# Down products of four feed-forward stages by Strassen's scheme, with the operand differences formed on GpSimd

## The reference, cut to what matters

```
def conv_ffn(x, w_up, conv_k, conv_b, w_down):          # layers of the first model
    h = x @ w_up                                         # 512 x 5632
    h = sum(hp[:, j:j + S] * conv_k[j] for j in range(CONV_W)) + conv_b
    a, b = jnp.split(h, 2, axis=-1)
    return (jax.nn.gelu(a, approximate=False) * b) @ w_down   # 512 x 2816 @ 2816 x 1024

def swiglu(xn, w_gate, w_up, w_down):                    # layers of the second model
    return (jax.nn.silu(xn @ w_gate) * (xn @ w_up)) @ w_down  # the same sizes
```

## Time and profile before

| | |
|---|---|
| time, median of 3 runs (lowest, highest) | 3466.81 us (3466.40, 3467.09) |
| span of the profiled execution | 3464.9 us |
| PE busy | 3404.4 us, 98% |
| DVE busy | 1870.3 us, 54% |
| ACT busy | 1401.5 us, 40% |
| POOL busy | 252.1 us, 7% |

### The profile page before, as it was taken

How to read it: one execution, slowest core, us unless ns; L and a number is a source line. 1 busy time by engine, 2 the same in 40 slices (tenths; PEclk the granted TensorE clock), 3 DMA queues, 4 the chain that set the end, 5 groups by cost and what they waited for, 6 DMA issues and landing times.

```text
span 3464.9 us, 41693 instructions
## 1 busy us (share of the span) xinstructions
PE 3404.4 (98%) x16871; PEld 2849.4 (82%) x16871; DVE 1870.3 (54%) x3030; ACT 1401.5 (40%) x2489; POOL 252.1 (7%) x319
## 2 busy tenths in 40 slices
PE   9999999999999999999999999999999999999999
PEld 8888888888888888888888777888888887888887
DVE  5644566646565545676455695553333696543332
ACT  4543233424235333334243554544232565543231
POOL 1300210000032002000001020100000000100000
PEclk9999999999999999999999999999999999999999
DMA  4111342322331123423232222412222302313222
GB/s 160 56 55 62 109 158 73 104 97 92 98 105 60 49 86 114 141 68 103 98 98 77 75 71 90 132 57 96 98 97 98 104 28 90 105 55 108 95 96 79
DMA packets 89330, 315.13 MB, mean 91 GB/s; under 512 B 10673, under 2 KB 11441, under 8 KB 88625
## 3 DMA queue, kind: packets, MB, share of 16 engines
q1 hardware_dynamic: 89136, 312.46, 27.4%
HBM read 308.23 MB, written 4.19 MB: 90 GB/s over the span
## 4 chain that ended last, share of the span: by engine, by line
PE 88%; DVE 7%; ACT 2%; POOL 2%; issue 1%; DMA 0%; SPq 0%; DVEq 0%; ACTq 0%; POOLq 0%
PE bk L1182 76%; PE bk L1276 3%; PE bk L1240 2%; PE bk L1250 1%; PE bk L1196 1%; DVE ar L2165 1%; DVE wl L1792 1%; DVE st L2163 1%; PE bk L1367 1%; PE bk L1365 1%; PE bk L1366 1%; POOL x L2354 1%; POOL st L2286 1%; DVE x L1821 0%; DMA wr<-in_wpk 0%
## 5 line engine op out<-in xcount | busy, mean ns | idle before, releaser
L1182 PE MATMUL bk<-xh,wh 128*128 128x512 f32 (+1 forms) x2216 | 837.8, 378 | 5.1 <-DVE xl L1805 5.1
L1182 PE MATMUL bk<-xh,wl 128*128 128x512 f32 (+1 forms) x2216 | 830.3, 375 | 0.0
L1182 PE MATMUL bk<-xl,wh 128*128 128x512 f32 (+1 forms) x2216 | 829.6, 374 | 0.0
L1792 DVE TENSOR_TENSOR wl<-wr,wh 128x1024 fp32r<-128x1024 f32 (+1 forms) x372 | 449.4, 1218 | 660.7 <-ACT wh L1438 659.7
L1438 ACT ACTIVATE wh<-wr 128x1024 fp32r<-128x1024 f32 (+1 forms) x372 | 385.8, 1046 | 706.4 <-PE bk L1182 653.6
L1182 PEld LDWEIGHTS bk<-xh,wh 128*128 128x128 f32 x2216 | 417.5, 188 | 78.6 <-DVE wl L1798 3.8
L1182 PEld LDWEIGHTS bk<-xh,wl 128*128 128x128 f32 x2216 | 417.2, 188 | 75.3
L1182 PEld LDWEIGHTS bk<-xl,wh 128*128 128x128 f32 x2216 | 417.6, 188 | 72.0
L1182 PE MATMUL bk<-wh,ah 128*128 128x512 f32 x1184 | 466.6, 394 | 4.5 <-DVE al L2250 2.9
L1182 PE MATMUL bk<-wh,al 128*128 128x512 f32 x1184 | 461.7, 390 | 0.0
L1182 PE MATMUL bk<-wl,ah 128*128 128x512 f32 x1184 | 461.3, 390 | 0.0
(11 more groups left out here) (276 smaller groups left out, 4095.5 us busy)
## 6 DMA issues: line engine op xcount, KB each, us to landing
wr<-in_wpk SPq DMA_DIRECT2D x540, 512.0 KB, 3.4
gb<-in_ln_g SPq DMA_DIRECT2D x6, 512.0 KB, 4.5
gb<-in_ln_b SPq DMA_DIRECT2D x6, 512.0 KB, 6.0
ar<-in_xT SPq DMA_DIRECT2D x8, 256.0 KB, 6.5
wr<-in_wpk SPq DMA_DIRECT2D x8, 256.0 KB, 6.0
ar<-in_memT SPq DMA_DIRECT2D x2, 1024.0 KB, 5.0
x<-in_x SPq DMA_DIRECT2D x4, 512.0 KB, 5.3
park<-x SPq DMA_DIRECT2D x4, 512.0 KB, 6.2
```

The source lines that it names most:

```text
L1182: i = pe.e.matmul(dst, lw, rw, start=g not in opened, stop=end)
L1792: dve.e.tensor_tensor(m.wl[:, s, a], m.wr[:, r, a], m.wh[:, s, a].bitcast(F32), ALU.subtract) \
```

## The change

The down products are done in four phases per stage instead of two, on pairs of chunks: phase 0 after three up groups on pairs 0 and 1, phase 1 after two more groups on pairs 2 to 4, phases 2 and 3 after three groups each on pairs 5 to 7 and 8 to 10. A pair's activations are four blocks of 128 features by 256 rows of x, its weights (now one DMA of 1 MB into a new buffer `wd`, 88 units of `wpk` less) four blocks of 128 by 512. `Seven` and `seven` make seven block products, named by their number in the order 1, 5, 2, 6, 3, 7, 4, where eight stood before. A product of all pairs of a phase is two parts: (q, 0) on the first two pairs, (q, 1) on the third (phase 0 has two pairs, so no second part). In the first three products all first parts come before the second ones. Each part is one unit of the five pairs `wh`, `wl`.

- `comb` (POOL, four instructions of 128x256 per pair) forms the sums and differences of the activations, `combo` (POOL, four of 128x512 per pair, T1 to T4) those of the weights.
- `hid_hi` (ACT) and `hid_lo` (DVE) split the seven left operands of a pair: 1792 columns for 1024 before.
- `sev` (DVE) adds a product's two banks to x after each product, two for product 7: 16 additions per phase, 64 per stage. Product 6 adds onto the bank of product 1, 7 onto that of 6, 3 onto that of 5, so PE waits for the additions of the earlier one (`AFTER`).
- In the last phase the products 2 and 3 finish row tiles 0 and 1, product 4 the tiles 2 and 3.

The core of the diff:

```diff
+LEFT = {1: 0, 5: 4, 2: 2, 6: 5, 3: 6, 7: 1, 4: 3}
+RIGHT = {1: 0, 5: 1, 2: 2, 6: 1, 3: 3, 7: 0, 4: 2}
+COMBO = {5: "T1", 6: "T2", 7: "T3", 4: "T4"}
+HOME = {1: "a", 6: "a", 7: "a", 5: "b", 3: "b", 2: "c", 4: "d"}
+PART = {1: ((0, 0),), 5: ((1, 1),), 2: ((0, 0),), 6: ((0, 1),), 3: ((0, 1),), 7: ((1, 1), (1, 0)), 4: ((1, 0),)}
+AFTER = {6: 1, 7: 6, 3: 5}
...
+    def seven(self, F):
+        n = len(F.chunks)
+        order = [(q, c) for c in range(n) for q in (1, 5, 2)] + [(q, c) for q in (6, 3, 7) for c in range(n)]
+        combos = {(1, 0): (("T2", 0), ("T3", 0)), (5, 0): (("T4", 0),), (2, 0): (("T2", 1), ("T3", 1)),
+                  (1, 1): (("T4", 1),)} if n > 1 else {}
...
+        for q, c in order:
+            product(q, c, (0, 1), True)
+            for name, cc in combos.get((q, c), ()):
+                for pair in F.chunks[cc] if cc < n else ():
+                    self.add("combo", F, name, pair)
+            if c == n - 1:
+                for tt in range(2):
+                    self.out_of(F, q, tt)
...
+            self.tick()
...
+                self.add("comb", si, pair)
+                self.soon += [("hid_hi", si, pair), ("hid_lo", si, pair)]
+            drive((self.seven(F), 1))
...
+    def smm(F, q, c, tiles, fin):            # PE
+        pe.wait_ge(*ev["w_lo", j])
+        for tt in tiles:
...
+            if q in AFTER:
+                pe.wait_ge(*ev["sev", F.si, F.ph, AFTER[q], tt])
+            for kk, pair in enumerate(F.chunks[c]):
+                pe.wait_ge(*ev["hid", F.si, pair])
...
+    def split_seven(j):                      # ACT
+        act.wait_ge(*ev["used", j - NR])
+        for pair in F.chunks[c]:
+            act.wait_ge(*ev[(COMBO[q], F.si, pair) if q in COMBO else ("d_sw", F.si, pair)])
...
+    def comb(si, pair):                      # POOL
+        for p in range(2):
+            pool.wait_ge(*ev["prod", si, 2 * pair + p])
...
+        pool.e.tensor_tensor(zx[:, 0, :], z[:, 1, :], z[:, 3, :], ALU.add).then_inc(*ev.up("pool_ev"))
+        own()
+        pool.e.tensor_tensor(zx[:, 1, :], zx[:, 0, :], z[:, 0, :], ALU.subtract).then_inc(*ev.up("pool_ev"))
+        pool.e.tensor_tensor(z[:, 1, :], z[:, 0, :], z[:, 1, :], ALU.subtract).then_inc(*ev.up("pool_ev"))
+        own()
+        pool.e.tensor_tensor(zx[:, 2, :], z[:, 2, :], zx[:, 1, :], ALU.subtract) \
+            .then_inc(*ev.up("pool_ev", ("comb", si, pair)))
+    def combo(F, name, pair):                # POOL
+        w = m.wd[:, F.pairs.index(pair)]
+        dst, x, y = {"T1": (1, 1, 0), "T2": (1, 3, 1), "T3": (0, 1, 0), "T4": (2, 2, 1)}[name]
...
+        pool.e.tensor_tensor(w[:, dst, :], w[:, x, :], w[:, y, :], ALU.subtract) \
+            .then_inc(*ev.up("pool_ev", (name, F.si, pair)))
```

More of the change, by code:

```diff
@@ L193, in __init__ @@
         self.last_gate, self.last_branch, self.conv_g = {}, {}, None
+        self.soon, self.part = [], None
         self.build()
+        self.raws = [j for j, d in enumerate(self.units) if d[0] != "seven"]
+        self.raw = {j: r for r, j in enumerate(self.raws)}
     def add(self, *item):
@@ L313, in leave @@
     def leave(self, t):
+        if self.part is not None:
+            self.out_of(self.part, 4, t - 2)
+            return
         self.add("ev", self.last_res, t)
@@ L595, in ffn @@
             self.add("gb_loads", si)
-        up, down = ("f_w_up", "f_w_down") if one else (None, "ffn_w_down_2")
+        up = "f_w_up" if one else None
         def ups(m):
@@ L605, in ups @@
             return self.gemm(G, self.ev(G), head=m == 0)
[L606 to L611, removed]
+        before = None
+        for ph, (made, pairs) in enumerate((((0, 1, 2), (0, 1)), ((3, 4), (2, 3, 4)), ((5, 6, 7), (5, 6, 7)),
+                                            ((8, 9, 10), (8, 9, 10)))):
+            F = Seven(si, ph, pairs, ph == 3)
+            loads = {0: ((1, 0), (1, 2)), 1: ((0, 0), (0, 1), (0, 2))}.get(ph, ((0, 1), (0, 3), (1, 1)))
+            diffs = {0: ((1, 3), (2, 0)), 1: ((0, 2), (0, 3), (1, 0))}.get(ph, ((0, 3), (1, 1), (1, 3)))
+            early = {(2, 1): "T2", (2, 2): "T3", (2, 3): "T4"} if ph == 0 else {}
+            for n, pair in enumerate(made):
+                for step, _ in enumerate(ups(2 * pair)):
+                    if (n, step) in loads:
+                        self.add("down_load", F, before, pairs[loads.index((n, step))], l)
+                    if (n, step) in diffs:
+                        self.add("combo", F, "T1", pairs[diffs.index((n, step))])
+                    if (n, step) in early:
+                        for one_of in pairs:
+                            self.add("combo", F, early[n, step], one_of)
+                    self.tick()
+                self.add("comb", si, pair)
+                self.soon += [("hid_hi", si, pair), ("hid_lo", si, pair)]
+            drive((self.seven(F), 1))
+            before = F
     def mixer2(self):
@@ L2407, in split @@
     def split(j):
-        if j + NRAW < len(sc.units):
+        if j in sc.raw and sc.raw[j] + NRAW < len(sc.raws):
             sp.wait_ge(*ev["w_lo", j])
-            weights(j + NRAW)
+            weights(sc.raw[j] + NRAW)
     def row(name, l, n):
@@ L2651 @@
     sc = Script(len(Script(None).units))
[L2652 removed]
+    arrays = lay_out(inputs, [sc.units[j] for j in sc.raws])
     nc = _bacc.Bacc("TRN2", target_bir_lowering=False, num_devices=1, dynamic_dma_scratch_size=1024)
```

229 lines of the change are left out of this document (177 added, 52 removed).

## The result

The changed kernel takes 3580.9 us, the median of 4 runs (3580.3 to 3585.1), for 3466.95 us before: 3.3% slower, ratio 1.033 with a 95% interval of 1.0316 to 1.0345. The forecast was 3574 us. The profiled execution has a span of 3579.1 us, 114.2 more than before.

What follows compares the result with a forecast made beforehand. The prediction took PE to bound the kernel: 59.8 us saved, against 114.6 lost in long phases, 23 in first phases and 29 at stage ends, +107 us on 3466.8, so 3574 us, range 3495 to 3610.

Steps and rivals of the forecast that it cites:

- What PE saves: Down products: 42 matmuls per pair of chunks for 48, 264 less at 0.2267 us each, 59.8 us saved.
- The chain in a long phase: Three-pair phases: POOL's sums and T2, ACT's copy, DVE's addition delay product 6 by 11.2 us (conv), 7.9 (gated); 114.6 in all.
- E: The time at which the last up group's matmuls end, ahead of a phase's down products; E+12.2 is 12.2 us later.
- two cases: Long phases: POOL and DVE keep each other out, 3574 us, chance 0.62; or they do not, 3509 us, 0.2.
- What the others get: Added work: DVE 65 us per stage, POOL 345 us in all, ACT some 10 us per stage; no engine bound on average.
- It costs nothing more: Wait of (1,1) for the last pair's low parts, done at E+13 to E+17 for E+8.2, lies inside product 6's loss.
- signs of being wrong: PE's wait before product 6 under 5 us in gated stages, longest wait at (1,1), or idle time in the up groups.
- The first phases: Two-pair phases: product 7 starts at E+20.8 for E+13.6, 7.2 us lost in a conv stage, 4.2 gated, 23 over four.
- The ends: Stage ends: DVE's queue before turned x of tile 0 delays the next stage 12.8 us twice, 3 after stage 8; 29 together.
- the first rival: Long phases: POOL and DVE don't hold each other up, 50 us lost there, 3509 us; chance 0.2.
- starved: First half of phases: DVE's weight pieces each wait out a POOL instruction, 54 us more, 3628 us; chance 0.08.
- The faster case: Start of product 6: POOL's chain ends by E+12.2 under the products ahead, saving kept in full, 3407 us; chance 0.08.

Runs made afterwards that it cites:

- keep-busy run: Changed kernel plus extra matmuls into an unread bank ahead of product part (1,1), 24 in a conv phase and 12 in a gated one: 3598.9 us.
- run with fills: Changed kernel with each weight difference on POOL replaced by two memsets of its destination, which read nothing from SBUF: 3527.8 us.
- last version: Kernel with late first-phase work and later tile 1 norm, plus (5,1) ahead of low parts, third pair's sums late, product 7's additions behind that norm: 3462.0 us.
- low parts right behind the sums: Kernel with sums on DVE and early differences, plus last pair's copies and low parts queued right behind its sums, last chunk's products ordered 1, 2, 5: 3485.1 us.

## Why the prediction was right, point by point

- *What PE saves.* 264 matmuls less, as counted. The 59.8 us hold in the sum.
- *The chain in a long phase.* Its steps hold, in the first long phase of stage 2: the sums on POOL begin at E+4.3 (E+4.05), take 3.4 us (2.8), T2 is there at E+19.6 (E+20.65), DVE's addition lets product 6 go at E+22.1 (E+23.4). The chain ends within 0.02 us of the same place in all six conv phases, and the keep-busy run shows it by itself. POOL and DVE keeping each other out was the choice that decided between 3574 and 3509. The run with fills shows it: 53 us, where the prediction's two cases stood 65 apart.
- *What the others get.* DVE's busy time rose by 303 us for the 260 of the sum, and POOL's by 444 for 345. The sums were of instructions by themselves; side by side they took longer. With the two fills in place of each difference DVE was busy 64 us less.
- *"It costs nothing more"*, of the wait at (1,1). This held, and so did its time (done at E+15.0, for E+13 to E+17). But two of the signs of being wrong in the prediction's last sentence came out all the same. The longest wait is at (1,1), 6.7 us, and ahead of product 6 PE waits 0 to 1.5 us in a conv stage and 0 to 1.3 in a gated one, not 5 or more. Both signs were badly made: PE's lateness at product 6 is what the chain sets, and the earlier wait and the slow matmuls behind it take up nearly all of it. The two chains end within 1.6 us of each other. So each of the two edits that shortened one chain gained less than its length, and only the kernels that shortened both came near the time of before.
- *The clock* stood in no term. Of the 46.6 us some 25 lie inside the long phases, between the wait at (1,1) and product 6, under T2's chain, and cost nothing there. Some 7 lie in the first phases, in part under the wait for product 7, and 7 behind the ends, where they are lost.
- *The first phases*: 29.3 for 23 us. In the conv stages the place was wrong. In stage 2 product 3 waits 3.9 us for the addition of product 5, whose weight part ahead waits for ACT's `hid_hi`; product 7 then starts at E+23.1 for E+20.8, behind slow matmuls and a wait of 1.6 us. In the gated stages the wait is at product 7 as forecast, 3.2 and 3.6 us for 4.2.
- *The ends*: 10.5 and 13.0 us for 12.8 twice, by DVE's queue as worked out. After stage 8 it is 8.1 for 3: ACT's two passes per tile over x, and its copies of the next weights, stand where the layer norm's work stands elsewhere, and I had no term for them.
- *The rivals.* Without the exclusion the first rival would have held, and the fills show what that would have been, 3528 and not 3509. The long phases lose 53 us in that run, where the rival had 50, though with the low parts at their end and not T2; the rest is the first phases (28 us for 23) and the ends with their slow matmuls. DVE was not starved: its first addition comes at E+21.3, sooner than in the sum, and the list of PE's waits names none for a weight part of these phases. The faster case was possible, but not with this order: it takes the sums off POOL, the differences ahead, the low parts first, and gives 0.16%.

The numbers missed by 7 us because errors of both signs met: the long phases 9 us less than worked out, the first phases 6, the ends 3 and the slow matmuls behind them 7 more. That much of the near hit is luck; the chain that carries most of the sum is not.

## What to carry to other kernels

A saving of matmuls by added operand sums is paid on the path from the last activation to the first product that needs it. Work out this path instruction by instruction, with the queues' order, before you count engine shares: every engine here had 39% of its time free or more, PE apart, and the change still lost 174 us for the 59.8 that it saved. Where two chains end close together, shorten both or expect little. And let DVE's instructions with two SBUF operands and POOL's that read SBUF stand at different times, or one of them outside the path: here it cost 53 us that they met on it.

## What the runs showed of the hardware

- *PE's granted clock after a wait.* Behind idle stretches of 3.5 us and more some of the next 14 matmuls of 512 columns always stood 0.427 us apart for 0.227, at a granted clock of 0.50, but their number changed from phase to phase: in the changed kernel 13, 9 and 6 behind the same wait of 6.7 us, in stage 2 and again in stage 5. Behind waits of 1.2 to 1.7 us none did. In between both were seen: 8 or 9 slow matmuls or none behind 1.9 us (last version) and 2.1 us (low parts right behind the sums), 7 to 14 or none behind 2.8 us (keep-busy run). A wait thus cost 0 to 3.0 us more than its length, and nothing more where another wait followed that the slow matmuls filled.
- *POOL's prices.* A subtraction of 128x512 floats took 1.27 us alone and up to 2.29 beside DVE, one of 128x256 took 0.74, a fill of 128x512 took 0.53 us and stretched none of DVE's 44 low parts of 1024 columns (1.215 to 1.222 us), one of which took 2.31 beside the differences.
- *Sums on DVE.* The same 128x256 sum takes DVE 0.43 us, and the four of a pair 1.7 us from start to end for 3.4 on POOL.
